# Second block: the first pair of scores and its softmax issued ahead of the banded heads' feeds, and the banded keys normed behind the second pair's reads

## The chip, the cores and the metric

One core of a Trainium2 chip runs the whole kernel. The metric is the device time of one execution in microseconds; of several runs the median is given. Times inside the kernel are those of one profiled execution, counted from the start of its span.

## The reference

Four transformer layers run one after the other over 256 tokens of width 1024: two of a "first block" (a gated linear recurrence beside sparse attention, and a feed-forward), then two of a "second block". The change is in the second block, of which this is the part that matters:

```python
h = rms_norm(x, g_mix)
proj = h @ w_in
c_q, c_kv, k_r, d_q, d_k, d_v, s_q, s_k, s_v, gate_logits = jnp.split(proj, offs, axis=-1)
q = (rms_norm(c_q, g_q_lora) @ w_uq).reshape(b, s, MLA_HEADS, MLA_NOPE + MLA_ROPE)
kv = (rms_norm(c_kv, g_kv_lora) @ w_ukv).reshape(b, s, MLA_HEADS, MLA_NOPE + MLA_V)
...
dq = rms_norm(d_q.reshape(b, s, 2, DIFF_HEADS, DIFF_QK), g_diff_q)
dk = rms_norm(d_k.reshape(b, s, 2, DIFF_HEADS, DIFF_QK), g_diff_k)
od = diff_attention(dq, dk, dv, positions, lam, slopes[WIN_HEADS:])
...
wq = rms_norm(s_q.reshape(b, s, WIN_HEADS, WIN_HEAD_DIM), g_win_q)
wk = rms_norm(s_k.reshape(b, s, WIN_KV_HEADS, WIN_HEAD_DIM), g_win_k)
o_win = window_attention(wq, wk, wv, positions, win_sink, slopes[:WIN_HEADS])
gates = jax.nn.sigmoid(gate_logits.reshape(b, s, N_BRANCH, D_MODEL))
```

There are 24 softmax items a layer, one for each map of 256 queries by 256 keys: items 0 to 7 are the differential heads, 8 to 15 the banded (window) heads, 16 to 23 the MLA heads.

## The kernel before

**Weights.** All weights come as a stream of units of 128 x 1024 floats through a ring of 7 slots. SyncE loads a unit into `raw` when the slot's former unit has been split. ScalarE rounds it to `w_hi` (L680), and VectorE or GpSimd forms the remainder `w_lo = raw - w_hi` (L684); of every seven units VectorE has five and GpSimd two (places 2 and 5 of the ring). TensorE then makes each product in three matmuls (`hi` by `hi`, `hi` by `lo`, `lo` by `hi`). ScalarE may round unit u when TensorE has begun unit u - 6. Each engine's program is one list in a fixed order, written by hand; `split.ahead(u)` puts into it the splitting of all units up to u + 6 that are not yet split. In the second block units 19 to 22 are the banded queries (`sq0` to `sq3`), 23 to 26 the banded keys and values (`skv0` to `skv3`), and from 27 on come the 24 gate tiles `gl0` to `gl23`.

**The stretch of the change.** TensorE feeds the latents, the differential queries, keys and values, the MLA up-projections (`uq`, `ukv`), then the banded queries and keys (`token_major`, L735). Then a software pipeline of items follows, here called steps. In step i TensorE computes the scores of two items (L1252, every second step), transposes the exps of item i - 2 (`turn2`, L1273), weighs the values by item i - 3 (`weigh2`, L1292), and forms gate tile i (`feature_major`, L718). In step 3 it also transposes the normed banded queries, in step 5 the normed banded keys (L1184).

VectorE subtracts the distance bias from the scores, which frees their bank (`item`, L2492), and takes the row maxima (L2497). ScalarE takes the exps (L1786). ScalarE copies the transposed exps of even items to SBUF (L573), VectorE those of odd items (L571), and ScalarE reads each gate tile (L1428).

The banded heads' norm goes from engine to engine: squares on ScalarE (`head_squares`, L1705), sums on VectorE (`head_means`, L2395), the root on ScalarE (`head_norms`, L1711 and L1712), and the scaling on VectorE (`head_scale`, L2403). `sq` is number 3 of these, `skv` number 4. The squares of the MLA heads are GpSimd's (L2775, and L2779 for the second token tile, which stands in its list behind the remainder of unit 26); VectorE sums them in steps 1 and 2 (L2534).

**Banks.** The eight PSUM banks are dealt out by a table. Banks 4 to 7 go round in the order of use. Here items 0 and 1 have banks 6 and 7, gl0 bank 4, gl1 bank 5, items 2 and 3 again 6 and 7, the turn of item 0 bank 4, gl2 bank 5, the turn of item 1 bank 6, the turns of the banded queries 7 and 4, and gl3 bank 5. A bank is written again only when its reader is done.

Of the kernel before, what the change touches and what calls it, by code (L numbers as in the profile page):

```python
# [20 lines left out]
ACT = mybir.ActivationFunctionType  # L21
# [4 lines left out]
S = 256  # L26
T = S // P
# [275 lines left out]
def program(nc, stream, x_in, consts_in, onehot_in, rb_in, flip_in, param1_in, rows1_in,  # L303
# [5 lines left out]
    with ctx:  # L309
# [241 lines left out]
        def stat_of(i):  # L551

            return 2 * (WIN + PAIRED[i - WIN] if WIN <= i < MLA else i)
# [145 lines left out]
        def _(pe):  # L699
# [458 lines left out]
            def second_block(at):  # L1158
# [15 lines left out]
                def pair_of(b0, n):  # L1174
                    return [[(bank[b0 + t][:, 0:n], 0, n)] for t in range(T)]
# [47 lines left out]
                for t in range(T):  # L1223
                    pe.wait_ge(*banks.free(at, f"ukv{t}"))
                    token_split(at, [uid["ukv"]], t, wide(0), c_t_hi, c_t_lo, 2, 1, D, True, True
                                ).then_inc(*banks.fills(at, f"ukv{t}"))
                pe.wait_ge(*banks.free(at, "sq"))
                feed([f"sq{k}" for k in range(4)], x_t_hi, x_t_lo, pair_of(0, 512), 2, 512, ["sq"])
                pe.wait_ge(*banks.free(at, "skv"))
                feed([f"skv{k}" for k in range(4)], x_t_hi, x_t_lo, pair_of(2, 256), 2, 256, ["skv"])  # L1230


                def scores_pair(i):

                    if i == 0:
                        pe.wait_ge(*banks.read(at, "dkt1"))
                        pe.wait_ge(*banks.read(at, "dkt0"))
                    elif i == WIN:
                        pe.wait_ge(*banks.read(at, "sqt0"))
                        pe.wait_ge(*banks.read(at, "sqt1"))  # L1240
                        pe.wait_ge(*banks.read(at, "skt"))
                    pe.wait_ge(*banks.free(at, f"s{i}"))
                    pe.wait_ge(*banks.free(at, f"s{i + 1}"))
                    n = i // 2 % 4
                    for t in range(T):
                        for half in range(2):
                            rows_of = slice(64 * half, 64 * half + 64)
                            if i < WIN:
                                q, k = dq_t[rows_of, n, :], dk_t[rows_of, n, :]
                            else:  # L1250
                                q, k = sq_t[rows_of, n, :], sk_t[rows_of, :]
                            mm = pe.matmul(bank[banks.bank(at, f"s{i + half}")][:, t * S:(t + 1) * S],  # L1252
                                           q[:, t * P:(t + 1) * P], k, start=True, stop=True)
                            if t == 1:
                                mm.then_inc(*banks.fills(at, f"s{i + half}"))

                def scores2(i):
                    pe.wait_ge(*banks.free(at, f"s{i}"))
# [46 lines left out]
                            mm = pe.transpose(b[0:96, k * S + t * P:k * S + (t + 1) * P], qk[:, t, 2 * n + k, :], ident)  # L1305
                    mm.then_inc(*banks.fills(at, f"mt{n}"))

                pe.wait_ge(*banks.read(at, "dqt0"))
                pe.wait_ge(*banks.read(at, "dqt1"))
                for i in range(ITEMS + 3):  # L1310
                    if i < MLA and i % 2 == 0:
                        scores_pair(i)
                    elif MLA <= i < ITEMS:
                        scores2(i)
                    if 2 <= i < ITEMS + 2:
                        turn2(i - 2)
                    if i >= 3:
                        weigh2(i - 3)
                    if i in MLA_TURNS:
                        if i == 9:  # L1320
                            pe.wait_ge(*c["mla_roped"](at, 1))
                        mla_turn(i - 9)
                        mla_turn(i - 8)
                    if i == 3:
                        heads_turned("sqt0", 3, sqn, 0, 2)
                        heads_turned("sqt1", 3, sqn, 2, 2)
                    elif i == 5:
                        heads_turned("skt", 4, skn, 0, 1)
                    if i < 24:
                        pe.wait_ge(*banks.free(at, f"gl{i}"))  # L1330
                        feature_major(at, uid[f"gl{i}"], bank[banks.bank(at, f"gl{i}")][:, 0:S], x_t_hi, x_t_lo, KT
                                      ).then_inc(*banks.fills(at, f"gl{i}"))
# [53 lines left out]
        def _(act):  # L1386
# [321 lines left out]
            def head_norms(at, n, count, scale=1.0 / 64):  # L1708
                act.wait_ge(*c["head_ms"](at, n))
                v = head_ms[:, 0:count]  # L1710
                step(act.activation(v, v, ACT.Ln, bias=eps6[:], scale=scale))  # L1711
                act.activation(v, v, ACT.Exp, scale=-0.5).then_inc(c["head_rstd"].sem, 1)  # L1712
# [7 lines left out]
            def second_block(at):  # L1720
# [42 lines left out]
                for h in range(2):  # L1763
# [3 lines left out]
                ins.then_inc(*banks.frees(at, "ukv0"))  # L1767
                act.activation(qk[:, 0, 8:16, 64:96], kr[:, 0, :].unsqueeze(1).broadcast_to([P, 8, 32]), ACT.Copy
                               ).then_inc(c["qk_act"].sem, 1)
                split.ahead(uid["sq3"])  # L1770
                head_squares(at, "sq", 3, 0, 512)
                head_norms(at, 3, 16)
# [2 lines left out]
                for t in range(T):  # L1775
                    act.activation(sv[:, t, :], bank[2 + t][:, P:2 * P], ACT.Copy)
                head_squares(at, "skv", 4, 2, P)
                head_norms(at, 4, 4)

                for i in range(ITEMS + 2):  # L1780
                    if i < ITEMS:
                        act.wait_ge(*c["z_ready"](at, i + 1))
                        for t in range(T):
                            source, scale = ((z2[:, i % 4, t * S:(t + 1) * S], 1.0) if i < MLA else
                                             (bank[banks.bank(at, f"s{i}")][:, t * S:(t + 1) * S], MLA_SCALE))
                            ins = act.activation(z2[:, i % 4, t * S:(t + 1) * S], source, ACT.Exp, scale=scale,  # L1786
                                                 bias=neg_max[:, stat_of(i) + t:stat_of(i) + t + 1],
                                                 accum_out=sums2[:, stat_of(i) + t:stat_of(i) + t + 1])
                        ins.then_inc(c["p_ready"].sem, 1)
                        if i >= MLA:  # L1790
                            act.wait_ge(*c["p_ready"](at, i + 1))
                            act.nop().then_inc(*banks.frees(at, f"s{i}"))
                    if i >= 2 and i % 2 == 0:
                        read_p2(act, at, i - 2)
                    if i == 3 or i == 4:
                        t = i - 3
                        act.wait_ge(*c["mla_ms"](at, t + 1))
                        v = mla_ms[:, 16 * t:16 * t + 16]
                        step(act.activation(v, v, ACT.Ln, bias=eps6[:], scale=1.0 / 96))
                        act.activation(v, v, ACT.Exp, scale=-0.5).then_inc(c["mla_rstd"].sem, 1)  # L1800
                    if i in MLA_TURNS:
                        read_mt(act, at, i - 9)
                    if i == 15:
                        act.wait_ge(*c["od_squared"](at, 1))
                        step(act.activation(od_ms, od_ms, ACT.Ln, bias=eps6[:], scale=1.0 / P))
                        act.activation(od_ms, od_ms, ACT.Exp, scale=-0.5).then_inc(c["od_rstd"].sem, 1)
                    if i == 18:
                        act.wait_ge(*c["sink_in"](at, 1))
                        act.activation(sink_part, sink_part, ACT.Exp).then_inc(c["sink_exp"].sem, 1)
                    if i == 3:  # L1810
                        read_heads(at, "sqt0", sq_t[:, 0:2, :], par2("g_sq"))
                    elif i == 5:
                        read_heads(at, "skt", sk_t[:], par2("g_sk"))
                    if i < 24:
                        split.ahead(uid[f"gl{i}"])
                        read_bank(at, f"gl{i}", gl[:, i, :], lambda b: b[:, 0:S])
                load_embedding(at)
                act.wait_ge(*banks.read(at, "gl23"))
                for m in range(2):
# [92 lines left out]
        def _(dve):  # L1912
# [510 lines left out]
            def second_block(at):  # L2423
# [44 lines left out]
                for h in range(2):  # L2468
# [4 lines left out]
                split.ahead(uid["ukv"])  # L2473
                dve.tensor_copy(qk[:, 1, 8:16, 64:96], kr[:, 1, :].unsqueeze(1).broadcast_to([P, 8, 32])
                                ).then_inc(c["qk_dve"].sem, 1)
                split.ahead(uid["sq3"])
                head_means(at, 3, 8)
                head_scale(at, "sq", 3, 8, 0, sqn)
                split.ahead(uid["skv3"])
                head_means(at, 4, 2)  # L2480
                head_scale(at, "skv", 4, 2, 2, skn)

                def item(i):
                    b = bank[banks.bank(at, f"s{i}")][:]
                    nm = neg_max[:, stat_of(i):stat_of(i) + 2]
# [16 lines left out]
                    else:  # L2502
                        step(dve.tensor_reduce(nm, b.rearrange("p (t s) -> p t s", t=T), AX.X, ALU.max))
                        dve.tensor_scalar(nm, nm, -MLA_SCALE, None, ALU.mult).then_inc(c["z_ready"].sem, 1)

                def rope(t):
                    dve.wait_ge(*c["mla_scaled"](at, t + 1))
                    x1, x2 = qk[:, t, :, 64:80], qk[:, t, :, 80:96]
# [10 lines left out]

                for i in range(ITEMS + 2):  # L2520

                    if i < MLA and i % 2 == 0:
                        item(i)
                        item(i + 1)
                    elif MLA <= i < ITEMS:
                        item(i)
                    if i >= 3 and i % 2 == 1:
# [431 lines left out]
```

## Time and profile before

| what | value |
|---|---|
| median of 3 runs | 1739.62 us (1739.42 to 1742.99) |
| the profiled execution | 1744.48 us, of which span 1742.7 us |
| TensorE busy | 1669.9 us |
| VectorE busy | 1172.9 us |
| ScalarE busy | 920.5 us |
| GpSimd busy | 443.5 us |
| TensorE's granted clock, mean | 0.987 of 2.4 GHz |

Engines in the profile: PE is TensorE's matmuls, DVE VectorE, ACT ScalarE, POOL GpSimd. In a timeline a row gives the start and the length in us, the engine, the line of the kernel, the operation, what it writes and reads, the shapes and how many instructions are merged in it; a bracket at the end gives the idle time before it and what ended it. Matmuls overlap by a tail, so that the start of the next one comes before the row's length is over.

### The profile page before, as it was taken

Reading aid. Unit: us, or ns where it says so; the run is one execution under the profiler, and the core shown is the slowest. Engines: PE = TensorE matmul, PEld = TensorE weight load, DVE = VectorE, ACT = ScalarE, POOL = GpSimd, SP = SyncE. Lnnn points to the kernel's source line nnn. Section 1 sums busy time; section 2 is a strip of 40 time slices with the busy share of each in tenths; the row PEclk is TensorE's granted clock in tenths of the full one; section 3 lists DMA queues with packets and bytes.
Section 4 is the critical chain, followed back from the end, with each engine's and each line's share of the span. In section 5 each row is a group of like instructions: output and inputs, shape, how many; then the busy total and the mean of one; then the engine's idle time right before and its main releaser. Section 6 shows DMA issues by size and latency. Waiting matters only on the chain.

```text
span 1742.7 us, 30149 instructions
## 1 busy us (share of the span) xinstructions
PE 1669.9 (96%) x11354; PEld 1521.1 (87%) x11354; DVE 1172.9 (67%) x1609; ACT 920.5 (53%) x1576; POOL 443.5 (25%) x184
## 2 busy tenths in 40 slices
PE   8989999999988999999999999999899999999997
PEld 6878799988987899978899989999788999899996
DVE  5687754558786644476784777656758856777667
ACT  5664544446645544455655564444665555554445
POOL 2222222222222222224511122222235211222222
PEclk9999999999999999999999999999999999999999
DMA  9442465556423655546323455665464333566653
GB/s 335 149 127 86 144 207 181 185 166 204 147 88 115 229 182 181 182 147 225 124 98 109 135 189 187 206 195 176 154 211 155 109 98 115 172 205 198 205 177 127
DMA packets 82563, 288.74 MB, mean 166 GB/s; under 512 B 9051, under 2 KB 11908, under 8 KB 81924
## 3 DMA queue, kind: packets, MB, share of 16 engines
q1 hardware_dynamic: 77352, 272.58, 47.5%
q10 hardware_dynamic: 5084, 14.37, 2.5%
q8 instruction: 91, 1.49, 0.3%
q14 instruction: 36, 0.29, 0.1%
HBM read 284.81 MB, written 2.11 MB: 165 GB/s over the span
## 4 chain that ended last, share of the span: by engine, by line
PE 61%; DVE 8%; ACT 3%; issue 2%; DVEq 0%; ACTq 0%
PE bank L718 30%; PE bank L735 24%; DVE w_lo L684 2%; PE bank L1292 2%; PE bank L1273 1%; PE bank L1264 1%; ACT w_hi L680 1%; PE bank L763 1%; PE bank L1252 1%; PE bank L1305 0%; DVE qk L2518 0%; PE bank L1184 0%; DVE decay_e L2065 0%; PE bank L908 0%; DVE z L2110 0%
## 5 line engine op out<-in xcount | busy, mean ns | idle before, releaser
L684 POOL TENSOR_TENSOR w_lo<-raw,w_hi 128x1024 fp32r<-128x1024 f32 x146 | 376.5, 2579 | 1221.0 <-ACT w_hi L680 1221.0
L684 DVE TENSOR_TENSOR w_lo<-raw,w_hi 128x1024 fp32r<-128x1024 f32 x364 | 555.8, 1551 | 158.2 <-ACT w_hi L680 156.8
L680 ACT ACTIVATE w_hi<-raw 128x1024 fp32r<-128x1024 f32 x510 | 519.9, 1051 | 109.5 <-PE bank L718 50.5
L718 PE MATMUL bank<-x_t_hi,w_hi 128*128 128x256 f32 x1984 | 326.9, 287 | 5.5 <-ACT gl L1428 3.0
L718 PE MATMUL bank<-x_t_hi,w_lo 128*128 128x256 f32 x1984 | 319.8, 284 | 0.0
L718 PE MATMUL bank<-x_t_lo,w_hi 128*128 128x256 f32 x1984 | 319.7, 284 | 0.0
L718 PEld LDWEIGHTS bank<-x_t_hi,w_hi 128*128 128x128 f32 x1984 | 279.1, 192 | 17.6 <-issue 5.4
L718 PEld LDWEIGHTS bank<-x_t_hi,w_lo 128*128 128x128 f32 x1984 | 274.7, 192 | 0.0
L718 PEld LDWEIGHTS bank<-x_t_lo,w_hi 128*128 128x128 f32 x1984 | 274.5, 192 | 0.0
L735 PE MATMUL bank<-w_hi,x_t_hi 128*128 128x512 f32 (+3 forms) x448 | 133.9, 382 | 9.6 <-issue 5.8
L735 PE MATMUL bank<-w_hi,x_t_lo 128*128 128x512 f32 (+3 forms) x448 | 131.4, 376 | 1.5 <-DVE x_t_lo L1951 1.5
L735 PE MATMUL bank<-w_lo,x_t_hi 128*128 128x512 f32 (+3 forms) x448 | 131.0, 375 | 0.0
L735 PE MATMUL bank<-w_hi,hs_hi 128*128 128x512 f32 x352 | 110.8, 396 | 3.4 <-ACT hs_hi L1864 3.4
L735 PE MATMUL bank<-w_lo,hs_hi 128*128 128x512 f32 x352 | 111.0, 397 | 0.0
L735 PE MATMUL bank<-w_hi,hs_lo 128*128 128x512 f32 x352 | 110.5, 395 | 0.0
L735 PEld LDWEIGHTS bank<-w_hi,x_t_hi 128*128 128x128 f32 x448 | 81.1, 191 | 28.9 <-issue 14.0
L735 PEld LDWEIGHTS bank<-w_hi,x_t_lo 128*128 128x128 f32 x448 | 82.3, 190 | 17.3 <-DVE x_t_lo L1951 3.4
L735 PEld LDWEIGHTS bank<-w_lo,x_t_hi 128*128 128x128 f32 x448 | 83.0, 190 | 14.3
L1860 ACT ACTIVATE gs<-cv 128x256 f32<-128x256 f32 x44 | 18.4, 418 | 143.3 <-DVE cv L2666 143.3
L735 PEld LDWEIGHTS bank<-w_hi,hs_lo 128*128 128x128 f32 x352 | 66.7, 189 | 16.0
L735 PEld LDWEIGHTS bank<-w_lo,hs_hi 128*128 128x128 f32 x352 | 66.2, 188 | 16.0
L2353 DVE TENSOR_TENSOR hs_lo<-hs,hs_hi 128x256 fp32r<-128x256 f32 x36 | 15.3, 425 | 91.0 <-ACT hs_hi L1643 91.0
(391 smaller groups left out, 2136.0 us busy)
## 6 DMA issues: line engine op xcount, KB each, us to landing
raw<-stream SPq DMA_DIRECT2D x511, 512.0 KB, 4.3
rows<-rows ACTq DMA_DIRECT2D x4, 1024.0 KB, 4.8
gain<-rows ACTq DMA_DIRECT2D x8, 512.0 KB, 4.9
hv_p<-hv_dram ACTq DMA_DIRECT2D x14, 256.0 KB
x<-x_in SPq DMA_DIRECT2D x2, 512.0 KB, 4.7
bias_r<-rev_dram SPq DMA_DIRECT2D x1, 1024.0 KB, 7.0
hv_dram<-hv ACTq DMA_DIRECT2D x2, 512.0 KB, 7.9
y_out<-x SPq DMA_DIRECT2D x2, 512.0 KB, 2.7
```

The source lines that it names most:

```text
L680: self.eng.activation(w_hi[:, i, :], raw[:, i, :], ACT.Copy).then_inc(hi_done.sem, 1)
L684: self.eng.tensor_tensor(w_lo[:, i, :], raw[:, i, :], w_hi[:, i, :].bitcast(F32), ALU.subtract).then_inc((lo_pool if self.part == "pool" e ...
L718: mm = pe.matmul(target, a[:, i, w0 + kt * P:w0 + (kt + 1) * P], b[:, k0 + kt, :], start=kt + k == 0, stop=k == 2 and kt == kts - 1)
L735: mm = pe.matmul(target, a[:, kt0 + j, t * P:(t + 1) * P], b[:, i, j * width + c0:j * width + c0 + cn], start=first and j + k == 0, stop=l ...
L763: mm = pe.transpose(b[:, k * P:(k + 1) * P], source[:, t, (4 * h + k) * P:(4 * h + k + 1) * P], ident)
L1252: mm = pe.matmul(bank[banks.bank(at, f"s{i + half}")][:, t * S:(t + 1) * S], q[:, t * P:(t + 1) * P], k, start=True, stop=True)
L1264: mm = pe.matmul(b[:, t * S:(t + 1) * S], mq_t[:, h, t * P:(t + 1) * P], mk_t[:, h, :], start=True, stop=True)
L1273: mm = pe.transpose(b[:, m * P:(m + 1) * P], z2[:, i % 4, m * P:(m + 1) * P], ident)
L1292: mm = pe.matmul(bank[b0 + t][:, o], p_t2[:, i % 2, m * P:(m + 1) * P], v, start=kk == 0, stop=kk == 1)
L1860: act.activation(gs2[:, i % 2, :], cv[:, i % 2, :], ACT.Gelu_apprx_tanh).then_inc(c["gate_silu"].sem, 1)
L2353: dve.tensor_tensor(hs_lo[:, i % TAIL, :], hs[:, i % 2, :], hs_hi[:, i % TAIL, :].bitcast(F32), ALU.subtract).then_inc(c["h_lo"].sem, 1)
```

## The change

On TensorE the scores of items 0 and 1 are issued behind the MLA up-projections and ahead of the feeds of the banded heads. On VectorE items 0 and 1 come ahead of the banded norms (and with them ahead of the remainders of units 25 and later). On ScalarE the exps of items 0 and 1 come ahead of the roundings of units 25 and later. The root of the banded keys' norm moves on ScalarE from before step 0 to the end of step 1, and their scaling on VectorE to behind items 2 and 3. No instruction is added or left out, and the table of banks is unchanged. `item_exp2` is the old code under a name.

```diff
 # TensorE
-                pe.wait_ge(*banks.free(at, "sq"))
-                feed([f"sq{k}" for k in range(4)], x_t_hi, x_t_lo, pair_of(0, 512), 2, 512, ["sq"])
-                pe.wait_ge(*banks.free(at, "skv"))
-                feed([f"skv{k}" for k in range(4)], x_t_hi, x_t_lo, pair_of(2, 256), 2, 256, ["skv"])
...
+                pe.wait_ge(*banks.read(at, "dqt0"))
+                pe.wait_ge(*banks.read(at, "dqt1"))
+                scores_pair(0)
+                pe.wait_ge(*banks.free(at, "sq"))
+                feed([f"sq{k}" for k in range(4)], x_t_hi, x_t_lo, pair_of(0, 512), 2, 512, ["sq"])
+                pe.wait_ge(*banks.free(at, "skv"))
+                feed([f"skv{k}" for k in range(4)], x_t_hi, x_t_lo, pair_of(2, 256), 2, 256, ["skv"])
...
-                pe.wait_ge(*banks.read(at, "dqt0"))
-                pe.wait_ge(*banks.read(at, "dqt1"))
                 for i in range(ITEMS + 3):
-                    if i < MLA and i % 2 == 0:
+                    if 0 < i < MLA and i % 2 == 0:
                         scores_pair(i)
 # ScalarE
+                item_exp2(0)
+                item_exp2(1)
                 split.ahead(uid["sq3"])
                 head_squares(at, "sq", 3, 0, 512)
                 head_norms(at, 3, 16)
...
                 head_squares(at, "skv", 4, 2, P)
-                head_norms(at, 4, 4)
 
                 for i in range(ITEMS + 2):
-                    if i < ITEMS:
...
+                    if 2 <= i < ITEMS:
+                        item_exp2(i)
...
                         read_bank(at, f"gl{i}", gl[:, i, :], lambda b: b[:, 0:S])
+                    if i == 1:
+                        head_norms(at, 4, 4)
 # VectorE
-                split.ahead(uid["sq3"])
-                head_means(at, 3, 8)
-                head_scale(at, "sq", 3, 8, 0, sqn)
-                split.ahead(uid["skv3"])
-                head_means(at, 4, 2)
-                head_scale(at, "skv", 4, 2, 2, skn)
...
+                item(0)
+                item(1)
+                split.ahead(uid["sq3"])
+                head_means(at, 3, 8)
+                head_scale(at, "sq", 3, 8, 0, sqn)
+                split.ahead(uid["skv3"])
+                head_means(at, 4, 2)
...
-                    if i < MLA and i % 2 == 0:
+                    if 0 < i < MLA and i % 2 == 0:
                         item(i)
                         item(i + 1)
+                        if i == 2:
+                            head_scale(at, "skv", 4, 2, 2, skn)
```

## Rows read from the trace of the kernel before

**Rows 1.** The page, span and busy time of each engine.

```profile
span 1742.7 us, 30149 instructions
PE 1669.9 (96%) x11354; PEld 1521.1 (87%) x11354; DVE 1172.9 (67%) x1609; ACT 920.5 (53%) x1576; POOL 443.5 (25%) x184
```

**Rows 2.** TensorE's timeline, first layer of the second block.

```profile
815.12 0.73 PE L735 MATMUL bank<-w_hi,x_t_hi 128*128 128x512 f32 x2
...
826.14 0.40 PE L735 MATMUL bank<-w_hi,x_t_hi 128*128 128x256 f32 x2
...
831.98 1.13 PE L1252 MATMUL bank<-dk_t,dq_t 64*128 64x256 f32 x8
...
840.24 1.14 PE L1252 MATMUL bank<-dk_t,dq_t 64*128 64x256 f32 x8 [1.18 <-DVE z L2492]
841.98 0.63 PE L1273 MATMUL bank<-consts,z 128*128 128x128 f32 x4 [0.61 <-ACT gl L1428]
844.09 0.94 PE L718 MATMUL bank<-x_t_hi,w_hi 128*128 128x256 f32 x4 [1.48 <-ACT gl L1428]
...
848.56 0.60 PE L1273 MATMUL bank<-consts,z 128*128 128x128 f32 x4
...
850.68 0.72 PE L718 MATMUL bank<-x_t_hi,w_hi 128*128 128x256 f32 x4
```

**Rows 3.** TensorE's timeline, second layer, the same places.

```profile
1333.95 0.74 PE L718 MATMUL bank<-x_t_hi,w_hi 128*128 128x256 f32 x4 [1.48 <-ACT gl L1428]
...
1336.93 0.60 PE L1273 MATMUL bank<-consts,z 128*128 128x128 f32 x4
...
1339.05 0.72 PE L718 MATMUL bank<-x_t_hi,w_hi 128*128 128x256 f32 x4
```

**Rows 4.** Windows: stretch, length, busy of PE, PEld, DVE, ACT, POOL, PEclk, DMA.

```profile
844.00:847.00 3.00, 2.91 (x15) 2.91 (x16) 2.73 (x3) 2.46 (x7) 0.01 (x1) 0.57 0.46 164
```

**Rows 5.** VectorE's timeline, first layer of the second block.

```profile
819.40 1.21 DVE L684 TENSOR_TENSOR w_lo<-raw,w_hi 128x1024 fp32r<-128x1024 f32 x1
...
822.28 1.67 DVE L684 TENSOR_TENSOR w_lo<-raw,w_hi 128x1024 fp32r<-128x1024 f32 x1 [1.67 <-ACT w_hi L680]
...
827.56 1.21 DVE L2395 TENSOR_REDUCE small<-sq 128x16 f32<-128x1024 f32 x1
829.39 1.29 DVE L2403 TENSOR_TENSOR sqn<-bank,small 128x512 f32<-128x512 f32 x2 [0.62 <-ACT small L1712]
...
832.24 4.28 DVE L684 TENSOR_TENSOR w_lo<-raw,w_hi 128x1024 fp32r<-128x1024 f32 x2 [0.19 <-ACT w_hi L680]
...
838.09 0.69 DVE L2492 SCALAR_TENSOR_TENSOR z<-dist,bank 128x512 f32<-128x512 f32 x1 [0.15 <-DVE skn L2403]
...
840.73 1.75 DVE L2534 TENSOR_REDUCE small<-mla_sq 128x16 f32<-128x1536 f32 x1
```

**Rows 6.** ScalarE's timeline, first layer of the second block.

```profile
829.27 3.88 ACT L680 ACTIVATE w_hi<-raw 128x1024 fp32r<-128x1024 f32 x4
...
833.37 0.44 ACT L1705 ACTIVATE sq<-bank 128x128 f32<-128x128 f32 x2
...
839.53 0.51 ACT L1786 ACTIVATE z<-z,small 128x256 f32<-128x256 f32 x1 [2.12 <-DVE small L2497]
...
840.53 1.04 ACT L680 ACTIVATE w_hi<-raw 128x1024 fp32r<-128x1024 f32 x1
...
844.92 0.59 ACT L573 ACTIVATE p_t<-bank 128x512 f32<-128x512 f32 x1
```

**Rows 7.** GpSimd's timeline, first layer of the second block.

```profile
819.61 3.26 POOL L684 TENSOR_TENSOR w_lo<-raw,w_hi 128x1024 fp32r<-128x1024 f32 x1 [1.41 <-ACT w_hi L680]
822.83 3.73 POOL L2779 TENSOR_TENSOR mla_sq<-qk 128x1536 f32<-128x1536 f32 x1
```

**Rows 8.** VectorE's and GpSimd's timelines, the last remainders of the kernel.

```profile
1737.92 4.50 DVE L684 TENSOR_TENSOR w_lo<-raw,w_hi 128x1024 fp32r<-128x1024 f32 x2
...
1738.40 2.95 POOL L684 TENSOR_TENSOR w_lo<-raw,w_hi 128x1024 fp32r<-128x1024 f32 x1 [10.41 <-ACT w_hi L680]
```

More of the change, by code:

```diff
@@ L1769, in second_block, with item_exp2 @@
                                ).then_inc(c["qk_act"].sem, 1)
+                def item_exp2(i):
+                    act.wait_ge(*c["z_ready"](at, i + 1))
+                    for t in range(T):
+                        source, scale = ((z2[:, i % 4, t * S:(t + 1) * S], 1.0) if i < MLA else
+                                         (bank[banks.bank(at, f"s{i}")][:, t * S:(t + 1) * S], MLA_SCALE))
+                        ins = act.activation(z2[:, i % 4, t * S:(t + 1) * S], source, ACT.Exp, scale=scale,
+                                             bias=neg_max[:, stat_of(i) + t:stat_of(i) + t + 1],
+                                             accum_out=sums2[:, stat_of(i) + t:stat_of(i) + t + 1])
+                    ins.then_inc(c["p_ready"].sem, 1)
+                    if i >= MLA:
+                        act.wait_ge(*c["p_ready"](at, i + 1))
+                        act.nop().then_inc(*banks.frees(at, f"s{i}"))
+                item_exp2(0)
+                item_exp2(1)
                 split.ahead(uid["sq3"])
@@ L1777, in second_block @@
                 head_squares(at, "skv", 4, 2, P)
-                head_norms(at, 4, 4)
                 for i in range(ITEMS + 2):
-                    if i < ITEMS:
[L1782 to L1792, printed above, removed]
+                    if 2 <= i < ITEMS:
+                        item_exp2(i)
                     if i >= 2 and i % 2 == 0:
```

## The prediction

> **What bounds the kernel now.** I read the page first: TensorE is busy for 1669.9 us of a span of 1742.7 [rows 1], so time is to be had only where TensorE stands still, and anything on another engine costs only when it makes TensorE stand still. The change touches one stretch in each layer of the second block, so I then read TensorE's timeline there. In the first layer the banded feeds run from 815.12, the first pair of scores is issued at 831.98, the gate tiles gl0 and gl1 follow, and then come three stalls: 1.18 us before the second pair of scores (bank of the first pair not yet read by VectorE, L2492), 0.61 before the first turn and 1.48 before gl2 (both wait for ScalarE's reads of the gate banks, L1428). gl3 begins at 850.68 [rows 2]. That is 3.27 us of stall a layer. The second layer shows the same stretch 489.86 later (1333.95 against 844.09), with the same 1.48 us stall; but from gl2 to the next turn it takes 2.98 us (1333.95 to 1336.93), the first layer 4.47 (844.09 to 848.56) [rows 2, 3]. The difference of 1.49 us is the clock: in 844 to 847 the granted clock is 0.57, so part of it ran at 1.2 GHz [rows 4]; the second layer's 2.98 is the time at 2.4 GHz. So at most 2 x 3.27 + 1.49 = 8.0 us are in reach. I use first-layer times below; gl3 begins at 850.68 there and, less the 489.86, at 849.19 in the second layer.
>
> **The unchanged parts.** No instruction is added or removed: the same matmuls, exps, sums and roundings run in another order, no DMA is issued anew, and the weight stream's queue (SyncE) is moved only by when slots come free. So the whole effect is in waits, and I replay the stretch with the durations of the rows: an operation starts when its engine is free and what it waits for has ended. Done for the order of before, this gives gl2 at 844.18 and gl3 at 849.27, where the second layer's rows, shifted, have 844.09 and 849.19: good to 0.1 us.
>
> **TensorE's part of the move.** The pair of scores (1.07 us: 1.13 of the row, less the tail that the next matmul overlaps) goes ahead of the feeds, which start 1.07 later and end 1.07 later; gl0 still starts at 833.0. Sum: nothing. Nothing is late for it either: the queries' and keys' turns that it reads were read out before the latents' products.
>
> **VectorE and ScalarE, the first pair.** VectorE comes to this place at 819.40, where it had a remainder before (w_lo, L684, 1.21 us when nothing is in its way) [rows 5]. It does item 0 and item 1 in 819.4 to 822.1 (1.41 from the start of an item to its maximum, by 838.09 to 839.53 of before less the signal; the second starts 1.33 after the first). ScalarE now waits for them: exp 0 in 820.8 to 821.9 and exp 1 in 822.1 to 823.2 (1.09 for one item, since the next operation starts 1.00 after it: 839.53, 840.53) [rows 6]. Behind these exps are queued the four roundings of units 25 to 28, the last two banded key units and gl0, gl1, which had nothing to wait for. They now run from 823.15, 0.97 each (3.88 for four) [rows 6], and end at 824.2, 825.2, 826.15 and 827.1.
>
> **What this sets off: the port.** VectorE's and GpSimd's remainders are not independent. VectorE's remainder of 1.21 us took 1.67 when it started at 822.28, while GpSimd was busy until 822.87: it ended 1.08 after that. GpSimd's square of the MLA heads (L2779), started at 822.83, ended at 826.56, 2.61 after VectorE's end at 823.95 [rows 5, 7]. So the two take turns, one whole instruction at a time. Who wins when VectorE has a second remainder right behind the first? At the kernel's end VectorE starts two remainders at 1737.92 and GpSimd one at 1738.40: GpSimd ends at 1741.35, VectorE's pair only at 1742.42, so GpSimd went between the two [rows 8]. I take that. The Trainium skill speaks against this change here: SBUF — State Buffer, section "Who interferes with whom", says a VectorE instruction with two SBUF inputs and a GpSimd one reading SBUF exclude each other, and issue order decides. By that rule the sum below is the same; the trace agrees.
>
> Before, VectorE's remainders were spread out, one per rounding. Now they come packed, with GpSimd's in between:
> - unit 25 on VectorE 824.2 to 825.45; unit 26 on GpSimd to 827.7 (2.25 after it gets its turn); unit 27 on VectorE to 828.8 (1.08); the MLA square on GpSimd to 831.4 (2.61; its code stands behind unit 26); unit 28 on VectorE to 832.5. Before, unit 28 was ready at about 827.6. TensorE needs units 25 to 28 at 830.1, 831.5, 833.0 and 835.9 (key units of 1.46 each, 826.14 to 831.98 for four [rows 2], ending at 833.0; then gl0): no stall, with 4.6, 3.8, 4.2 and 3.4 us to spare. That is what hides the delay; more of it and TensorE waits for units.
> - The banded queries' means: 832.4 to 833.6 (1.21), 0.62 for ScalarE's root, the scaling (1.29) to 835.55; before it ended at 830.68 [rows 5]. So this is 4.9 us late. ScalarE stood behind its norm meanwhile: its next four roundings start at 834.1 rather than 829.27.
> - unit 29 on VectorE 835.7 to 836.9; 30 on GpSimd to 839.15; 31 on VectorE to 840.25. ScalarE's rounding of unit 33 ends at 834.1 + 4.54 (start of four roundings to the end of the keys' squares, 829.27 to 833.81) + 1.0 = 839.75 [rows 6], so GpSimd asks for its turn 0.4 us before 840.25 and has it to 842.5; unit 32 ends on VectorE at 843.6. Before, it ended at 836.52 [rows 5].
> - the keys' means (0.4) to 843.9, the MLA sums (1.74, [rows 5]) to 845.55, item 2's subtraction to 846.15, its maximum to 846.9. Before, its subtraction ended near 843.2 (840.73 + 1.75 + 0.69).
>
> **The keys' norm behind the reads.** ScalarE's norm of the keys leaves the chain ahead of the gate reads, where it held ScalarE from 833.81 until VectorE had summed the keys, behind 836.52 [rows 5, 6]. That is the gain: gl0's bank is read at 840.05 and gl1's at 841.3, gl2 starts at 841.35 instead of 844.09. The stall before the second pair of scores is gone too (its banks are read at 821).
>
> **Where the stall goes.** gl2 ends at 844.3. The next turn (L1273) writes the bank of item 2, which VectorE frees only at 846.15: TensorE waits 2.0 us. Then the weighing (L1292) waits for ScalarE's read of the first p: exp of item 2 in 846.9 to 848.0, the read (0.59, [rows 6]) to 848.5: TensorE waits 1.8 us more. From there the weighing and the queries' turns take 1.7 (2.12 from the start of the turn, 848.56 to 850.68 [rows 2], of which the turn is 0.44). gl3 begins at 850.26. Stalls: 0.3 + 0.8 + 2.0 + 1.8 = 4.9. The same replay of the order of before has 3.8 (the 3.27 and small gaps that the trace doesn't mark), so about 1.07 more. After gl3 each step is timed by TensorE again, and the later wait for the rotated MLA heads moves with it, since the rotation starts behind a p that TensorE turned.
>
> Sum, without any half clock: first layer 850.26 - 850.68 = -0.4, second 850.26 - 849.19 = +1.07, together +0.65 us.
>
> **The clock.** Before, one of two layers fell to 1.2 GHz after stalls of 1.18, 0.61 and 1.48 with 1.14 and 0.63 of work between them; it cost 1.49. Now TensorE has 0.46 us of work from 844.3 to 848.56. That is emptier, so I take one to two falls: bounds 0 and 2 x 1.49 = 2.98, I take 1.95 (the half-speed stretch may partly lie in the stall). The Trainium skill, TensorE: Matmul & The Clock Gate, section "What's actually happening", ties the low clock to an idle stretch; by it, stalls broken by work as here would cost nothing; the first layer's row disagrees.
>
> Sum: +0.65 + 1.95 = +2.6 us on the profiled execution (1744.48, span 1742.7). I put it on the median of 1739.62, which is 4.9 below the profiled time, since the stalls are the same in kind: 1742.2.
>
> **The rivals.**
> - No fall of the clock in either layer: +0.65, 1740.3. For it: the second layer of before did not fall in the same stalls. Against: the stall is emptier now. 0.12. (It is also what the Trainium skill's page on the clock gate, named above, would have.)
> - VectorE gets one of the two disputed turns (unit 28 ahead of the MLA square, or unit 32 ahead of unit 33, a margin of only 0.4 us). Each is worth about 2.3 to 2.6 us of VectorE; gl3 begins at about 847.7: -3.0 and -1.5, sum -4.5, 1735.1, with a fall 1736.6. Against: [rows 8]. 0.14.
> - It does all it says: both disputed turns go to VectorE, so item 2 is early enough and no stall is left. -8.0, 1731.6. Only possible if the port does not order the packed remainders as I read it. 0.15.
> - Slower beyond doubt: the clock falls in both layers at full price, and the late read of the first p makes one more wait of about 0.7 a layer in the next step, as VectorE has both the MLA sums of the second tile and the p copy behind item 3. +0.65 + 2.98 + 1.4 = +5.0, 1744.6. It decides once GpSimd's scaling of the MLA heads meets unit 34's remainder ahead of item 4. 0.16.
> - My forecast, 1741.0 to 1743.8: 0.43.
>
> **How the numbers follow.** 0.2% is 3.5 us, about what a measurement here can tell from no change: 1736.1 and 1743.1. Faster: 0.15 + 0.08 of the half gain = 0.23. Slower: 0.16 + 0.11 of my own case = 0.27. Same: 0.50. The range 1733.5 to 1744.6 leaves out the full gain (0.15) and the top of the slow case (0.05). The likeliest case's own range is 1741.0 to 1743.8.
>
> **What the profile after would show.** Right: no stall before the second pair of scores; gl2 near 841.4; then about 2 us of TensorE waiting for VectorE's z (L2492) before the second turn, and about 1.8 for ScalarE's p (L573) before the first weighing; VectorE's remainders of units 27, 28, 31 and 32 of 2.6 to 3.8 us; the queries' means near 832.4; gl3 near 850.3 or, at half clock, 851.5. Wrong: remainders of 1.2 us each, the queries' means before 830, gl3 before 848. The prediction falls with the order at the port: it carries some 4.9 us of VectorE's time a layer.

## The result and the profile after

The changed kernel is slower. Its median is 1748.81 us (1748.58 to 1751.48, 5 runs) against 1740.17 (1739.42 to 1742.99, 5 runs) for the kernel before, a ratio of 1.0043 with a 95% interval of 1.0032 to 1.0054: about +7.5 us by the ratio (the medians lie 8.6 apart). A second time, beside twenty runs of before, it was 1747.51 against 1743.03, 1.0027 (1.0018 to 1.0037). The forecast was 1742.2, in the range 1733.5 to 1744.6.

The page after, span and busy time, against [rows 1]: TensorE is busy 1.5 us longer, the span is 4.3 us longer.

```profile
span 1747.0 us, 30149 instructions
PE 1671.4 (96%) x11354; PEld 1522.1 (87%) x11354; DVE 1178.4 (67%) x1609; ACT 919.6 (53%) x1576; POOL 442.9 (25%) x184
```

TensorE's timeline in the first layer of the second block, where [rows 2] are those of before. This execution came to the place 1.70 us sooner (the copy of the rotary keys on VectorE starts at 817.50, before at 819.20), so 1.70 is to be added to set a time beside one of before or of the prediction.

```profile
837.14 1.14 PE L1246 MATMUL bank<-dk_t,dq_t 64*128 64x256 f32 x8
838.32 0.63 PE L1276 MATMUL bank<-consts,z 128*128 128x128 f32 x4
839.45 0.74 PE L718 MATMUL bank<-x_t_hi,w_hi 128*128 128x256 f32 x4 [0.50 <-ACT gl L1429]
...
844.59 0.63 PE L1276 MATMUL bank<-consts,z 128*128 128x128 f32 x4 [2.02 <-DVE z L2492]
846.92 2.05 PE L1295 MATMUL bank<-dv,p_t 128*128 128x128 f32 x8 [1.70 <-ACT p_t L573]
848.75 1.92 PE L1184 MATMUL bank<-consts,sqn 128*128 128x128 f32 x8
850.32 1.20 PE L718 MATMUL bank<-x_t_hi,w_hi 128*128 128x256 f32 x4
...
854.54 1.14 PE L1246 MATMUL bank<-dk_t,dq_t 64*128 64x256 f32 x8
```

The stall before the second pair of scores is gone and gl2 starts at 841.15 on the scale of before. Then come 2.02 us of waiting for VectorE's subtraction of item 2 and 1.70 us for ScalarE's copy of the first p. Behind them the eight matmuls of the weighing last 2.05 us and the eight turns of the queries 1.92. In the kernel before the same two groups last 1.06 and 1.04 us:

```profile
849.00 1.06 PE L1292 MATMUL bank<-dv,p_t 128*128 128x128 f32 x8
849.89 1.04 PE L1184 MATMUL bank<-consts,sqn 128*128 128x128 f32 x8
```

The second layer (in [rows 3] before) has the same two stalls and the same slow matmuls behind them:

```profile
1337.11 0.63 PE L1276 MATMUL bank<-consts,z 128*128 128x128 f32 x4 [2.02 <-DVE z L2492]
1339.43 2.05 PE L1295 MATMUL bank<-dv,p_t 128*128 128x128 f32 x8 [1.70 <-ACT p_t L573]
1341.28 1.92 PE L1184 MATMUL bank<-consts,sqn 128*128 128x128 f32 x8
```

The windows over these places (columns as in [rows 4]; the third column from the right is the granted clock):

```profile
848.00:851.00 3.00, 3.00 (x16) 3.00 (x16) 1.67 (x3) 2.09 (x8) 1.51 (x1) 0.50 0.00 0
851.00:854.00 3.00, 3.00 (x20) 3.00 (x20) 2.33 (x2) 1.04 (x1) 2.92 (x2) 0.67 0.00 0
1338.00:1341.00 3.00, 1.56 (x7) 1.59 (x8) 2.81 (x5) 3.00 (x10) 0.00 (x0) 0.50 0.32 127
1341.00:1344.00 3.00, 3.00 (x16) 3.00 (x15) 1.67 (x4) 2.09 (x6) 1.99 (x1) 0.50 0.01 3
```

TensorE ran at 1.2 GHz in both layers, and still did while it was busy without a gap (3.00 of 3.00 us). A stretch at 1.2 GHz is called a fall of the clock below. The one of before is shorter; here is a window around each, first that of before, then the two of the changed kernel:

```profile
844.25:848.00 3.75, 3.75 (x20) 3.75 (x21) 2.48 (x3) 2.21 (x6) 0.00 (x0) 0.54 0.39 140
846.00:853.25 7.25, 6.33 (x30) 6.36 (x31) 5.77 (x7) 5.13 (x13) 3.68 (x2) 0.53 0.02 10
1337.50:1344.75 7.25, 5.55 (x29) 5.34 (x27) 5.73 (x9) 5.93 (x15) 2.74 (x1) 0.53 0.20 79
```

The mean clock is nearly the same in all three, and the windows of the changed kernel are almost twice as long. In finer windows TensorE works at 1.2 GHz from 844.5 to 847.9 before, 3.4 us, and in the changed kernel from the weighing on, to 853.0 and to 1344.5: 6.1 and 5.1 us.

VectorE's timeline, where [rows 5] are those of before:

```profile
822.52 1.22 DVE L684 TENSOR_TENSOR w_lo<-raw,w_hi 128x1024 fp32r<-128x1024 f32 x1 [2.11 <-ACT w_hi L680]
824.42 6.37 DVE L684 TENSOR_TENSOR w_lo<-raw,w_hi 128x1024 fp32r<-128x1024 f32 x2 [0.67 <-ACT w_hi L680]
830.71 1.21 DVE L2402 TENSOR_REDUCE small<-sq 128x16 f32<-128x1024 f32 x1
832.54 1.29 DVE L2410 TENSOR_TENSOR sqn<-bank,small 128x512 f32<-128x512 f32 x2 [0.62 <-ACT small L1713]
...
835.38 6.48 DVE L684 TENSOR_TENSOR w_lo<-raw,w_hi 128x1024 fp32r<-128x1024 f32 x2 [0.19 <-ACT w_hi L680]
841.79 0.40 DVE L2402 TENSOR_REDUCE small<-sq 128x4 f32<-128x256 f32 x1
842.12 1.74 DVE L2544 TENSOR_REDUCE small<-mla_sq 128x16 f32<-128x1536 f32 x1
843.77 0.67 DVE L2492 SCALAR_TENSOR_TENSOR z<-dist,bank 128x512 f32<-128x512 f32 x1
```

And GpSimd's, where [rows 7] are those of before:

```profile
823.51 2.50 POOL L684 TENSOR_TENSOR w_lo<-raw,w_hi 128x1024 fp32r<-128x1024 f32 x1 [7.02 <-ACT w_hi L680]
825.96 3.74 POOL L2789 TENSOR_TENSOR mla_sq<-qk 128x1536 f32<-128x1536 f32 x1
834.48 2.98 POOL L684 TENSOR_TENSOR w_lo<-raw,w_hi 128x1024 fp32r<-128x1024 f32 x1 [4.78 <-ACT w_hi L680]
837.98 2.80 POOL L684 TENSOR_TENSOR w_lo<-raw,w_hi 128x1024 fp32r<-128x1024 f32 x1 [0.52 <-ACT w_hi L680]
```

Two remainders of 1.2 us each take 6.37 us, since GpSimd's unit 26 goes ahead of the first and its MLA square (ends at 829.70) goes between them; the next two take 6.48 with units 30 and 33 of GpSimd in the same places. So item 2 is subtracted at 843.77, that is 845.47 on the scale of before.

**A measure for the stretch.** From here on a layer's stretch is the time from VectorE's copy of the rotary keys (L2481 here, L2474 before) to TensorE's first turn of MLA heads (L1308 here, L1305 before). It leaves out what varies elsewhere in the run. Before it is 819.20 to 881.37, 62.17 us, and 1309.06 to 1369.73, 60.67. After it is 817.50 to 882.20, 64.70, and 1310.01 to 1374.28, 64.27. The sum of both layers grew by 6.1 us, which lies in the interval of the result (5.6 to 9.4 us).

### The profile page after: what moved, and what is told of

The parts are those of the page before. It is cut to its first block, busy times and chain, and to the rows that moved or that the text cites. A ratio compares the mean times of both kernels' runs of the same rounds, so it can differ in the third digit from the quotient of the medians.

```text
span 1747.0 us, 30149 instructions
## 1 busy us (share of the span) xinstructions
PE 1671.4 (96%) x11354; PEld 1522.1 (87%) x11354; DVE 1178.4 (67%) x1609; ACT 919.6 (53%) x1576; POOL 442.9 (25%) x184
## 3 DMA queue, kind: packets, MB, share of 16 engines
q8 instruction: 91, 1.49, 0.3%
## 4 chain that ended last, share of the span: by engine, by line
PE 62%; DVE 8%; ACT 2%; issue 2%; DVEq 0%; ACTq 0%
PE bank L718 30%; PE bank L735 25%; DVE w_lo L684 3%; PE bank L1295 2%; PE bank L1276 1%; PE bank L1267 1%; ACT w_hi L680 1%; PE bank L1246 1%; PE bank L763 1%; PE bank L1308 0%; PE bank L1184 0%; PE bank L908 0%; DVE qk L2526 0%; PE bank L916 0%; DVE z L2117 0%
## 5 line engine op out<-in xcount | busy, mean ns | idle before, releaser
L684 DVE TENSOR_TENSOR w_lo<-raw,w_hi 128x1024 fp32r<-128x1024 f32 x364 | 562.0, 1568 | 158.7 <-ACT w_hi L680 157.3
```

The source lines that it names most:

```text
L684: self.eng.tensor_tensor(w_lo[:, i, :], raw[:, i, :], w_hi[:, i, :].bitcast(F32), ALU.subtract).then_inc((lo_pool if self.part == "pool" e ...
```

## The experiments

Each experiment is set against runs of the kernel before that were made beside it. Their median was 1742.23 for c1 and e1 to e3 (29 runs), 1742.84 for e4 to e7 (29) and 1743.03 for c2, e8 and e9 (20), which is about 3 us above the 1739.62 of its first three runs. So the ratio counts, and beside it the stretch, which is read from one trace of each kernel.

**The kernel before again (c1).** No edit.

> The kernel before, run against itself, for a second trace and the spread. My theory of the result (call it port and clock): the change makes gl3 begin about 1.1 us later in each layer of the second block, and TensorE then falls to 1.2 GHz in both layers, at 2.5 to 2.9 us each; a usual run of before has no stretch at 1.2 GHz there, and the first layer's in its first trace was an exception. It expects a ratio within 0.1% of 1, and gl2 to the next turn in about 3.0 us in both layers. Rival (noise): stretches at 1.2 GHz come and go anywhere, and the measured +7.5 us is partly theirs. It expects runs spread over 5 us or more, and at least one stretch at 1.2 GHz here in the trace.

Measured: 1741.78, ratio 1.0002 (0.9993 to 1.0011), runs of 1739.16 to 1745.59. The stretch is 62.16 us in the first layer and 60.67 in the second, as in the first trace. Theory and rival each have a part right: the ratio is 1, but the runs are spread over 6.4 us, and the first layer's fall was not an exception. Both traces of before have one fall here, of 1.49 us, in the first layer.

**The gate tile twice (e1).** The first pass counts the unit as begun, the second reports the bank as filled.

```diff
-                        feature_major(at, uid[f"gl{i}"], bank[banks.bank(at, f"gl{i}")][:, 0:S], x_t_hi, x_t_lo, KT
-                                      ).then_inc(*banks.fills(at, f"gl{i}"))
+                        if i == 2:
+                            feature_major(at, uid["gl2"], bank[banks.bank(at, "gl2")][:, 0:S], x_t_hi, x_t_lo, KT)
+                        feature_major(at, uid[f"gl{i}"], bank[banks.bank(at, f"gl{i}")][:, 0:S], x_t_hi, x_t_lo, KT,
+                                      begin=i != 2).then_inc(*banks.fills(at, f"gl{i}"))
```

> The changed kernel, with gate tile gl2's 24 matmuls issued twice, so that TensorE works where it waited for item 2's bank; the result is the same. The second pass takes 2.9 us and ends near 847.2 on the first-layer scale, and the weighing still waits for ScalarE's p until 848.5. Port and clock: gl3 begins at the same 850.3, but the clock does not fall (or rarely), so the time drops by about 5 us, from 1748.8 to about 1743.5, although each layer has 2.9 us more work on TensorE. Rival (the loss is all schedule): nothing is won, 1748.8 or up to 2 us more.

Measured: 1743.15, ratio to before 1.0009 (1.0000 to 1.0018), while the changed kernel has 1.0043 and 1.0027. TensorE's timeline, first layer:

```profile
841.32 0.60 PE L1276 MATMUL bank<-consts,z 128*128 128x128 f32 x4
842.93 1.13 PE L1295 MATMUL bank<-dv,p_t 128*128 128x128 f32 x8 [1.01 <-ACT p_t L573]
843.90 1.04 PE L1184 MATMUL bank<-consts,sqn 128*128 128x128 f32 x8
844.69 0.72 PE L718 MATMUL bank<-x_t_hi,w_hi 128*128 128x256 f32 x4
```

The wait for item 2's bank is filled, the weighing still waits for ScalarE's p, and the weighing and the turns take 1.13 and 1.04 us. The stretch is 61.86 and 61.87. With 24 more matmuls a layer it is 2.8 and 2.4 us shorter than in the changed kernel. This splits the loss: 61.9 against 60.67 is what the order costs, 1.2 us a layer, and the rest, 5.2 us in all, is TensorE at 1.2 GHz. The first layer's rows say the same without the stretch: from the weighing to gl3 it takes 1.76 us here and 3.40 in the changed kernel, and gl3 up to the next scores 3.05 and 4.22, together 2.8 us. The rival (all schedule) falls.

**GpSimd's square first (e2).**

```diff
                 split.ahead(uid["sq0"])
-                split.ahead(uid["sq1"])
                 pool.wait_ge(*c["qk_dve"](at, 1))
                 pool.tensor_tensor(mla_sq[:, 1], qk[:, 1], qk[:, 1], ALU.mult).then_inc(c["mla_squared"].sem, 1)
+                split.ahead(uid["sq1"])
```

> The changed kernel, with GpSimd's square of the MLA heads' second tile ahead of unit 26's remainder, not behind it, so that it doesn't come between VectorE's remainders of units 27 and 28. Port and clock: it runs by 821.5, unit 28 is split 2.6 us earlier, the queries' means begin near 829.8, and gl3 begins near 847.7 on the first-layer scale (850.3 in the changed kernel): -2.6 us a layer, and stalls of 0.5 and 1.8 instead of 2.0 and 1.8, so fewer falls of the clock: 1737 to 1741. Rival (the exps alone hold ScalarE up, the port doesn't matter): within 1 us of 1748.8.

Measured: 1740.07, ratio 0.9992 (0.9983 to 1.0001). The stretch is 59.32 and 59.31, 2.6 us under the 61.9 of schedule and 5.4 and 5.0 under the changed kernel. One instruction of another engine, moved on a queue that the change did not touch, takes the loss back. The wait before the second turn is 0.34 instead of 2.02, that for ScalarE's p is 1.70 as in the changed kernel, and the clock does not fall. The rival falls.

**The exps in their old place (e3).**

```diff
-                item_exp2(0)
-                item_exp2(1)
                 split.ahead(uid["sq3"])
...
-                    if 2 <= i < ITEMS:
+                    if i < ITEMS:
                         item_exp2(i)
```

> The changed kernel, with ScalarE's exps of items 0 and 1 back at their old places (head of steps 0 and 1); scores, items and the keys' norm stay moved. Port and clock: the roundings of units 25 to 28 come one by one as TensorE frees their slots, VectorE's and GpSimd's remainders don't meet in a pack, and no stall is left between gl1 and gl3: gl3 begins near 845.4 on the first-layer scale, 3.8 us ahead of before, 4.9 ahead of the changed kernel, with no stretch at 1.2 GHz: about 1732.5, 8 us under before. Rival (the early items on VectorE or the late keys' norm are what costs): 1746 or more.

Measured: 1732.06 (1730.85 to 1732.88), ratio 0.9944 (0.9932 to 0.9957). VectorE's timeline, first layer, which came to the copy of the rotary keys at 815.51:

```profile
818.34 6.98 DVE L684 TENSOR_TENSOR w_lo<-raw,w_hi 128x1024 fp32r<-128x1024 f32 x3
825.25 1.21 DVE L2400 TENSOR_REDUCE small<-sq 128x16 f32<-128x1024 f32 x1
...
829.92 4.30 DVE L684 TENSOR_TENSOR w_lo<-raw,w_hi 128x1024 fp32r<-128x1024 f32 x2 [0.18 <-ACT w_hi L680]
...
836.32 0.69 DVE L2490 SCALAR_TENSOR_TENSOR z<-dist,bank 128x512 f32<-128x512 f32 x1
```

The queries' means start 9.74 us after that copy (13.21 in the changed kernel), and item 2's subtraction 20.81 after it (26.27). TensorE has no stall between gl1 and gl3, and the stretch is 56.87 and 56.86 us. Three of the four moves of the change (scores, items, keys' norm) win about 10 us; with the fourth, the two exps ahead of four roundings in ScalarE's list, there is a loss instead.

**Both turns at the port (e4).** As e2, and GpSimd waits with unit 33 until VectorE has done unit 32 (`gl5`):

```diff
                 for u in range(uid["sq2"], uid["gl2"]):
+                    if u == uid["gl0"]:
+                        pool.wait_ge(*lo_taken(at, uid["gl5"]))
                     split.ahead(u)
```

> The changed kernel with both disputed turns at the port taken from GpSimd: its square of the second MLA tile runs ahead of unit 26's remainder, and its remainder of unit 33 waits until VectorE has done unit 32's. The exps stay ahead of the roundings. Port and clock: replayed from the rows, no stall is left ahead of gl3, the stretch from the copy of the rotary keys to the first MLA turn is 56.9 us as with the exps in place (60.7 before, 59.3 with the square first alone), no fall of the clock in it: 1732 to 1733. Rival (the exps ahead of the roundings cost something by ScalarE alone, which the port does not explain): 1736 or more.

Measured: 1733.35, ratio 0.9946 (0.9926 to 0.9965), the stretch 57.13 in both layers, no fall in it. VectorE's timeline, the same pairs of remainders as in the changed kernel:

```profile
824.75 3.82 DVE L684 TENSOR_TENSOR w_lo<-raw,w_hi 128x1024 fp32r<-128x1024 f32 x2 [0.67 <-ACT w_hi L680]
...
833.17 4.29 DVE L684 TENSOR_TENSOR w_lo<-raw,w_hi 128x1024 fp32r<-128x1024 f32 x2 [0.19 <-ACT w_hi L680]
```

3.82 and 4.29 us instead of 6.37 and 6.48. The exps are where the change put them, so ScalarE is as late as there; only GpSimd's two turns between VectorE's remainders are gone. Of the 5.0 us a layer between the schedules of the changed kernel and of e3 (61.9 and 56.87) this takes back 4.8, and the falls of the clock go too. The harm of the early exps goes by the port, up to 0.3 us a layer.

**The keys' norm alone (e5).** The kernel before, with `head_norms(at, 4, 4)` at the end of ScalarE's step 1 and `head_scale(at, "skv", ...)` behind items 2 and 3, as in the diff of the change.

> The kernel before with one part of the change: the root of the keys' norm behind gl1's read, the scaling behind items 2 and 3. Port and clock: the stall before the second pair of scores (1.2 us) goes, those before the first turn and gl2 (0.6 and 1.5) stay; the stretch is 59.3 us against 60.7: -1.3 us a layer and now and then a fall less: 1738 to 1740. Rival (the late keys' norm costs, since items 2 and 3 and the keys' turn meet later): 1742 or more.

Measured: 1739.58, ratio 0.9985 (0.9973 to 0.9997). The stretch is 60.83 and 60.80, with stalls of 0.52 and 1.48 and a fall in each layer. That is the expected 59.3 plus a fall of 1.5 each: this part alone wins 1.3 us a layer of schedule, and in the second layer, which did not fall before, the clock takes that back. The part does no harm. The stalls here are hardly larger than those of e2 (0.34 and 1.70, with the turn between them), where the clock did not fall: the two waits alone do not tell whether it does.

**All but the keys' norm (e6).** The changed kernel with those two lines back in their old places.

> The changed kernel without the move of the keys' norm: only the scores, items and exps go ahead. Port and clock: one stall of 3.8 us before the first turn (ScalarE waits for the keys' sums, which stand behind the packed remainders) and 0.5 before gl2; gl3 begins 0.3 us earlier than in the changed kernel, the stretch is 61.4 us plus a fall of the clock: 1743 to 1748. Rival (the late norm is the part that costs): 1740 or less.

Measured: 1745.95, ratio 1.0018 (1.0006 to 1.0030), the stretch 62.54 and 62.57. One stall, 3.65 us, and a slow start of gl2 behind it:

```profile
840.95 0.64 PE L1276 MATMUL bank<-consts,z 128*128 128x128 f32 x4 [3.65 <-ACT gl L1429]
842.08 1.22 PE L718 MATMUL bank<-x_t_hi,w_hi 128*128 128x256 f32 x4 [0.48 <-ACT gl L1429]
```

So there is a loss without the norm's move, and the rival (1740 or less) falls, but the loss is smaller: the two stretches are 2.3 us longer than before, against 6.1 with the move. From gl2 to the second turn it takes 4.17 us in the first layer and 4.19 in the second, against 2.97 in the first layer of e7, which has no fall, so a fall costs 1.2 us here and the schedule is 61.3. Beside the early exps the late norm thus adds 0.5 us of schedule a layer and 2.8 us of slow clock in all.

**Scores and items only (e7).** e3 with the keys' norm in its old place too.

> Only the scores on TensorE and items 0 and 1 on VectorE go ahead; exps and the keys' norm stay. Port and clock: stalls of about 0.7 and 1.5 us before the first turn and gl2, gl3 about 1.2 us earlier than before, the stretch 59.5 us: 1739 to 1741. With the exps in place and the norm moved it was 1732.1, so the norm's move is then worth about 7 us together with this. Rival (the norm's move adds nothing once the exps are in place): 1733.

Measured: 1742.31, ratio 0.9997 (0.9985 to 1.0009), the stretch 59.83 and 61.30, the second with a fall. I had 1739 to 1741, a little too fast: the stalls before the first turn and gl2 were 1.18 and 1.48, not 0.7 and 1.5. Its two layers have the same stalls, and the clock fell in one alone. Against e3 the norm's move is worth about 9 us by the ratios (0.9997 and 0.9944), 3.0 and 4.4 us in the two stretches. Without falls the norm's move alone wins 1.3 us a layer (e5), scores and items alone 0.8 (e7), both together 3.8 (e3): each needs the other. The rival (nothing added) falls.

**The changed kernel again (c2).** No edit.

> The changed kernel once more, for a second trace. Port and clock: the stretch from the copy of the rotary keys to the first MLA turn is 61.9 us of schedule (60.7 before) plus a fall of the clock in each layer, of 2.4 to 2.9 us, in nearly every run, since TensorE waits 3.7 us with one turn between: ratio 1.003 to 1.005. Rival (the falls in both layers of the first trace were chance): at least one layer without a fall, and a ratio of 1.002 or less.

Measured: 1747.51, ratio 1.0027 (1.0018 to 1.0037), a little under the expected 1.003 to 1.005. The stretch is 64.70 and 64.22 us, a fall in both layers again, as long and as dear as in the first trace. So the falls belong to the change, and the rival falls. The two intervals of the ratio overlap between 1.0032 and 1.0037.

**The exps behind the roundings (e8).**

```diff
-                item_exp2(0)
-                item_exp2(1)
                 split.ahead(uid["sq3"])
+                item_exp2(0)
+                item_exp2(1)
```

> The changed kernel with ScalarE's exps of items 0 and 1 one place later: behind the roundings of units 25 to 28, still ahead of the queries' squares. Port and clock: the roundings come one by one again; the queries' squares are 2 us late, and one stall of 1.2 us is left before the first weighing: the stretch is 58.1 us, 2.5 under before, 6.3 under the changed kernel with its falls; 1735 to 1737. Rival (any exp ahead of the queries' norm brings the pack back): 1742 or more.

Measured: 1737.03, ratio 0.9964 (0.9952 to 0.9976), the stretch 58.52 and 58.54 with one stall of 1.42. I had 58.1 and 1.2, so 0.4 too little a layer. One line further down in ScalarE's list, the same early exps win 6 us instead of losing as much. GpSimd's unit 33 still goes between VectorE's remainders of units 31 and 32 here (6.51 us for the pair), the turn that e4 takes away.

**Before, with gl1 twice (e9).** The edit of e1 on the kernel before, for tile gl1.

> The kernel before with gate tile gl1's 24 matmuls issued twice, 2.9 us of work in the place of the stalls of 1.2 and 0.6 us and some of the next. Port and clock: gl2 starts where it did or up to 0.2 us later (ScalarE's reads decide), and the first layer no longer falls to 1.2 GHz: the stretch is 60.7 to 61.2 us in both layers, against 62.2 and 60.7 before: within 0.1% of before, or up to 1 us faster. Rival (the first layer's 1.5 us is not from idling, but from its place in the run): 62.2 us or more remain in the first layer.

Measured: 1739.94, ratio 0.9987 (0.9978 to 0.9996). The stretch is 60.69 and 60.66: the first layer no longer falls, and the second is unchanged. Work that nobody needs made the kernel before about 2 us faster (0.7 to 3.8).

## Why the prediction was wrong

The schedule was right step by step. On the scale of before (times after plus 1.70):

| step | predicted | measured |
|---|---|---|
| unit 25's remainder starts | 824.2 | 824.22 |
| units 27 and 28 done, the MLA square between them | 832.5 | 832.49 |
| queries' scaling done | 835.55 | 835.53 |
| unit 32 done, unit 33 ahead of it | 843.6 | 843.56 |
| gl2 starts | 841.35 | 841.15 |
| second turn, after 2.0 of waiting | 846.3 | 846.29 |
| first weighing, after 1.8 of waiting | 848.56 | 848.62 |

The disputed turns at the port went to GpSimd, as read from [rows 8]; e2 and e4 show what they carry. Without falls gl3 begins 31.18 us after the copy of the rotary keys (e1, 844.69 less 813.51); 850.26 less 819.20 is 31.06. The term "+0.65 us" is thus right to 0.3: 2 x 1.2 less the 1.49 of before is +0.9.

The step that failed is **the clock**: "I take one to two falls: bounds 0 and 2 x 1.49 = 2.98, I take 1.95". It measured 5.2 us (64.70 and 64.27 against 61.9). The mechanism was named and the number of falls (two) was within it, but I took the price of before's fall for the most that one can cost. That fall held 3.4 us of TensorE's work, all in gl2 [rows 2, 4], and cost 1.49. Here the clock stayed low about twice as long: a part of it lay in the wait, as I had allowed for, but the weighing, the turns and the first half or third of gl3, 6.1 and 5.1 us, ran at 1.2 GHz, at 2.8 and 2.4 us a layer. Why the low clock lasted longer here than before stays open. The sum with the measured terms is 2.4 - 1.49 + 5.2 = +6.1, which the stretches show; with 1.95 it was +2.6. That is 3.5 of the 6.6 us between 1742.2 and 1748.81.

The other 3.1 us are the base, nearly as large a part. I set the sum on the median of three runs, 1739.62, though the profiled execution had 1744.48; the three later sets of before, 78 runs, had medians of 1742.2 to 1743.0. With +6.1 on these it is 1748.3 to 1749.1, where the changed kernel's medians were 1748.8 and 1747.5.

The rival "slower beyond doubt" had the right sign and nearly the size (+5.0, where the stretches have +6.1), but in part by luck: it too took 1.49 a fall, and its second mechanism did not happen: no further wait of 0.7 us came up in the next step. The rival without falls is refuted by both traces. The Trainium skill, TensorE: Matmul & The Clock Gate, section "What's actually happening", puts the low clock behind an idle stretch; read as pure idling, which I did, that gave this rival. The trace does not bear out that reading: a turn of 0.63 us (four transposes) lay between waits of 2.02 and 1.70, and the clock fell all the same. "It does all it says" was wrong for this kernel and came true in e3 and e4. I had priced it at -8.0, from the stalls that the trace marks; e3's two stretches are 9.1 us shorter than before (113.7 against 122.8). That is 2 x 3.8 + 1.49, with the 3.8 us of stall a layer that the replay counted, small gaps included.

## What to carry to other kernels

Moving an instruction ahead on one engine's fixed list delays everything that it is moved past: here two exps held up four roundings, and the rounded units then reached VectorE and GpSimd in a pack, where the two engines exclude each other. Replay the list of each engine with the durations of the trace before such a move, the engines that it does not touch included. Here that gave the changed kernel's two long waits to 0.1 us and the stretches of e4 to e8, falls aside, to 0.4 us, though e7's first stall was 1.18 and not 0.7; it also found the place one line further down. Where TensorE's waits lie close together, price the clock with them, and not by an earlier fall: one fall can last longer than another. Matmuls of no use in the place of a wait show how much of a loss is clock.

## What the runs showed of the hardware

- VectorE's remainder (two inputs in SBUF) and GpSimd's take turns by whole instructions, and a GpSimd instruction that waits goes between two of VectorE's that follow each other: pairs of 6.37 and 6.48 us that take 3.82 and 4.29 when GpSimd has only the turn ahead of them. The Trainium skill says the first part in SBUF — State Buffer, section "Who interferes with whom"; the trace agrees.
- TensorE fell to 1.2 GHz after waits of 2.02 and 1.70 us with 0.63 us of work between them, in both layers of both traces of the changed kernel, after 3.65 and 0.48 in both layers of e6, and after 0.52 and 1.48 in both of e5. It did not after 0.34 and 1.70 (e2), nor after 0.50 and 1.01 (e1). After 1.18 and 1.48 it fell in one layer of e7 and not in the other, and after 1.18, 0.61 and 1.48 in the first layer of both traces of before and not in the second. So the waits of TensorE that a trace marks do not settle it. The 1.2 GHz then lasted into work without a gap.
- A fall cost 1.5 us in the kernel before, with 3.4 us of work at 1.2 GHz, and 2.8 and 2.4 in the changed one, with 6.1 and 5.1: a little under half of that work's time.
- 24 matmuls of no use in the place of a wait made a kernel faster: ratio 0.9987 (0.9978 to 0.9996) on before.
